# One expert step of a fused decoder trunk: transposes behind both down units, slot weights in the activations, a scatter of split values

## The chip, the cores and the metric

The kernel runs on one core of a Trainium2 chip. TensorE (PE in the profile, PEld for its weight loads) multiplies, VectorE (DVE) and ScalarE (ACT) work element by element, GpSimd (POOL) and SyncE (SP) do small things and issue transfers. The engines run each its own list of instructions in order and wait for one another through semaphores. The metric is the device time of one execution in microseconds, the median of several runs.

## The reference, cut to what matters

A decoder trunk of two layers over 256 tokens of 1024 channels. Each layer is a token mixer and a channel mixer; the channel mixer of the second layer picks two of eight experts for each token. Only this last part is changed:

```python
def moe_swiglu(h, router_w, w_gate, w_up, w_down):
    logits = (h @ router_w).astype(jnp.float32)
    top_val, top_idx = lax.top_k(logits, TOP_K)
    probs = jax.nn.softmax(top_val, axis=-1)
    combine = jnp.sum(jax.nn.one_hot(top_idx, N_EXPERTS, dtype=jnp.float32) * probs[..., None], axis=-2)
    out = jnp.zeros_like(h)
    for e in range(N_EXPERTS):
        out = out + combine[..., e:e + 1].astype(h.dtype) * swiglu(h, w_gate[e], w_up[e], w_down[e])
    return out
```

An expert has 3584 hidden channels: gate and up are 1024 x 3584, down is 3584 x 1024, all float32.

## The kernel before, in words

All weights stream from memory in units of 1 MB (128 x 2048 float32) into six slots of `raw`. A weight is used as a sum of two fp32r values: ScalarE writes the high half (`moe_hi`, L730), VectorE the rest (`moe_lo`, L1110), and TensorE multiplies high by high, high by low and low by high. Three places hold split units in the expert stage, so the high half of unit w waits until TensorE has consumed unit w-3 (`act.wait_ge(consumed, w - SPLIT)`).

One expert is one step (`expert_step` on each engine), and it has 42 units. The hidden channels are cut into seven tiles of 512 (FT = 7). A tile has two gate units, two up units (`gate_up`, L1617, 12 matmuls of 512 columns each) and two down units (`down`, L1632, 12 matmuls too). The order is: units 0 to 3 are gate and up of tile 0; units 4 to 7 are gate and up of tile 1, units 8 and 9 down of tile 0; and so on up to units 38 and 39, down of tile 5; units 40 and 41 are down of tile 6. In the code, `tile(step, r, ...)` issues gate and up of one tile and down of the tile before it.

A step has up to 128 slots, the tokens that chose the expert. `select` (L1184) builds a 0/1 matrix `sel` of tokens by slots and a matrix `sel_w` with the router's weights in it. `gather` (L1652) multiplies the tokens by `sel` into two banks of PSUM; ScalarE (`input_high`, L812) and VectorE (`split_input`, L1256) split the result into `xe_hi` and `xe_lo`. For each tile ScalarE writes Silu of the gate (`silu_tile`, L780), VectorE multiplies it by the up result (`multiply`, L1244), TensorE transposes the product (`turn`, L1642, four transposes into bank 4), and the two engines split it again (`tile_high`, L807, `split_tile`, L1249) for the down units.

At the end of a step, TensorE transposes `sel_w` (`turn_selection`, L1660), ScalarE copies it and the result of the expert (`expert_result`, L819 and L821), and two units into the next step `scatter` (L1670) multiplies the result by the turned selection, in float32, into four banks; VectorE adds them to the output (`add_result`, L1264). In each tile, TensorE's order is

```python
down(step, k + 4, 1 - odd, 0, t - 1, first=first, rounds=rounds)
turn(step, odd, t)
down(step, k + 5, 1 - odd, 1, t - 1, rounds=rounds)
```

ScalarE's order in a tile is high halves 0 and 1 of its six units, `tile_high`, high halves 2 and 3, `silu_tile`, high halves 4 and 5. VectorE's is low halves 0 and 1, `split_tile`, low halves 2 to 5, `multiply`.

Of the kernel before, what the change touches and what calls it, by code (L numbers as in the profile page):

```python
# [29 lines left out]
P = 128  # L30
# [141 lines left out]
C_RS = A_CONST + 4 * P  # L172
C_RT = C_RS + T
C_MOD = C_RT + T
# [7 lines left out]
def program(nc, x_t, vecs, glr_w, a2, router, stream, experts, out_t):  # L182
    with ExitStack() as ctx:
# [93 lines left out]
        y_e = area(A_GATES + 4096, D)  # L277
        silu_e = [area(A_GATES + 5120 + 512 * i, 512) for i in range(2)]
        act_e = [area(A_SQ + 512 * i, 512) for i in range(2)]
        sel, sel_w, sel_t = area(A_SK, T), area(A_SK + 256, T), area(A_SK + 512, T)  # L280
# [12 lines left out]
        list_f, hits = area(A_GQ + 156, 8), area(A_GQ + 164, 8)  # L293
        router_sb = area(A_GQ + 256, KC, N_EXP)
        index = sb("index", [P, 2, 8], U32)
        xe_hi, xe_lo = split_area(0, KC * P), split_area(1024, KC * P)
        ae_hi = [split_area(4096 + 1024 * b, 512) for b in range(2)]
# [61 lines left out]
        ye_copied, scattered, moe_added = sem("expert_y_copied"), sem("scattered"), sem("moe_added")  # L359
        sel_zeroed, sel_w_ready = sem("selection_zeroed"), sem("weighted_selection_ready")  # L360

# [160 lines left out]
        def _(act):  # L522
# [259 lines left out]
            def expert_step(step, expert, first=False):  # L782
# [26 lines left out]
            def input_high(step, half):  # L809

                act.wait_ge(gathered, step * 2 + half + 1)
                act.activation(xe_hi[:, 512 * half:512 * half + 512], (bank[7], bank[4])[half][:, :],  # L812
                               ACT.Copy).then_inc(xe_hi_done, 1)
# [25 lines left out]
        def _(dve):  # L839
# [353 lines left out]
            dve.memset(sel_w, 0.0).then_inc(sel_zeroed, 1)  # L1193
# [29 lines left out]
            select(0, sel, chosen_f, sel_ready)  # L1223
            link(dve.tensor_scalar(places[:, :, 8:16], ranks, float(P), None, ALU.subtract))
# [15 lines left out]
            def multiply(step, k, odd, t, rounds=0):  # L1240
# [3 lines left out]
                dve.tensor_tensor(act_e[odd], bank[2 * odd + 1][:, :], silu_e[odd],  # L1244
                                  ALU.mult).then_inc(act_done, 1)
# [5 lines left out]
            def split_input(step, half):  # L1251

                src = (bank[7], bank[4])[half]
# [3 lines left out]
                                  ALU.subtract).then_inc(xe_split, 1)  # L1257

# [7 lines left out]
            def expert_step(step, expert, first=False):  # L1266
                for k in range(3 if first else 0, 4):
                    moe_lo(step, k)
                add_result(step)
                dve.wait_ge(sel_turned, step + 1)  # L1270
                select(column_of(step), sel_w, weights_f, sel_w_ready)
                moe_lo(step, 4)
# [6 lines left out]
                select(column_of(step + 1), sel, chosen_f, sel_ready)  # L1279
# [5 lines left out]
            def tile(step, r, rounds, t, whole):  # L1285


                if whole:
                    moe_lo(step, 4 + 6 * r, rounds)
# [11 lines left out]
            add_result(over_steps(dve, expert_step))  # L1301
# [4 lines left out]
        def _(pe):  # L1306
# [297 lines left out]
            pe.wait_ge(sel_zeroed, 1)  # L1604
# [40 lines left out]
            def gather(step, half):  # L1645
# [3 lines left out]
                for c in range(4):  # L1649
                    for t in range(2):  # L1650
                        at = D * t + P * (4 * half + c)
                        mm = pe.matmul((bank[7], bank[4])[half][:, P * c:P * c + P],  # L1652
# [4 lines left out]
            def turn_selection():  # L1657

                for t in range(2):
                    mm = pe.transpose(bank[7][:, P * t:P * t + P], sel_w[:, P * t:P * t + P], ident)  # L1660
# [12 lines left out]

            def expert_step(step, expert):
# [35 lines left out]
            pe.wait_ge(xe_split, 1)  # L1710
            turn_selection()
# [95 lines left out]
```

## Time and profile before

| | |
|---|---|
| runs | 1996.08, 1994.54, 1990.96 us; median 1994.54 |
| span of the profiled execution | 1994.1 us |
| its mean granted TensorE clock | 0.962 |
| TensorE busy | 1868.0 us, 94% |
| VectorE busy | 1549.3 us, 78% |
| ScalarE busy | 1174.3 us, 59% |
| read from memory | 522.65 MB |
| the expert stage | from about 946 us to 1974 us of the span, eight steps |

The span is the time from the first to the last instruction of one execution; no time of that execution other than its span is given, and it is 0.4 us under the median of the runs. Matmuls overlap one another, so the start of one after another tells more than their durations.

### The profile page before, as it was taken

What the parts mean: (1) busy time and instruction counts of PE and PEld (TensorE: products, weight loads), DVE (VectorE), ACT (ScalarE), POOL (GpSimd) and SP (SyncE); (2) the same over time, 40 slices, a digit from 0 to 9 for tenths busy, and PEclk for the clock granted to TensorE, in tenths of its full rate; (3) what the DMA queues carried; (4) which work ended last, traced back from release to release, by engine and by line L of the source; (5) the groups of instructions that cost most, each with busy time, mean ns of one, the idle gap of its engine ahead of it and who ended that gap; (6) DMA issues with size and microseconds to landing.
All of it is one profiled execution on the core that took longest, in us unless ns stands there. A gap on an engine that the chain in (4) does not pass through costs nothing.

```text
span 1994.1 us, 29410 instructions
## 1 busy us (share of the span) xinstructions
PE 1868.0 (94%) x10996; PEld 1648.5 (83%) x10997; DVE 1549.3 (78%) x1274; ACT 1174.3 (59%) x987; POOL 196.4 (10%) x185
## 2 busy tenths in 40 slices
PE   4979998799989899997999999999999999999997
PEld 3979998799988898996888888887888878888786
DVE  6967966877656558676888888888888888888886
ACT  3347554533334476453676766767767767676674
POOL 0461601000002705010000000000000000000000
PEclk7979999899999899997999999999999999999999
DMA  8944434588634333351798998989989889898892
GB/s 351 360 167 163 171 126 169 189 322 328 259 129 148 128 120 114 129 188 64 277 368 305 369 345 328 364 317 355 364 308 364 336 337 368 304 368 336 336 364 90
DMA packets 72380, 524.81 MB, mean 263 GB/s; under 512 B 8096, under 2 KB 8224, under 8 KB 8560
## 3 DMA queue, kind: packets, MB, share of 16 engines
q1 hardware_dynamic: 72144, 523.50, 69.6%
q8 instruction: 55, 0.90, 0.2%
q0 software_dynamic: 160, 0.23, 0.0%
q14 instruction: 21, 0.17, 0.0%
HBM read 522.65 MB, written 1.05 MB: 263 GB/s over the span
## 4 chain that ended last, share of the span: by engine, by line
PE 34%; DVE 14%; ACT 5%; issue 2%; DVEq 0%; ACTq 0%
PE bank L1617 18%; DVE w_lo L1110 11%; PE bank L1632 9%; ACT w_hi L730 4%; DVE arena L1244 2%; PE bank L1642 2%; PE bank L1652 2%; PE bank L1670 2%; PE bank L1351 1%; PE bank L1328 1%; PE bank L1587 0%; DVE arena L901 0%; DVE w_lo L851 0%; DVE arena L923 0%; DVEq L1242 0%
## 5 line engine op out<-in xcount | busy, mean ns | idle before, releaser
L1110 DVE TENSOR_TENSOR w_lo<-raw,w_hi 128x2048 fp32r<-128x2048 f32 x224 | 512.9, 2290 | 83.7 <-ACT w_hi L730 62.1
L730 ACT ACTIVATE w_hi<-raw 128x2048 fp32r<-128x2048 f32 x224 | 428.5, 1917 | 127.7 <-PE bank L1632 80.0
L1351 PE MATMUL bank<-acts,w_hi 128*128 128x256 f32 x2080 | 396.1, 292 | 19.6 <-DVE acts L914 11.8
L1351 PEld LDWEIGHTS bank<-acts,w_hi 128*128 128x128 f32 x2080 | 338.0, 200 | 24.8 <-issue 14.6
L1351 PE MATMUL bank<-acts,w_lo 128*128 128x256 f32 x1040 | 301.4, 290 | 0.0
L1617 PE MATMUL bank<-acts 128*128 128x512 f32 x1248 | 300.7, 390 | 0.0
L1617 PE MATMUL bank<-w_hi,acts 128*128 128x512 f32 x960 | 297.9, 392 | 1.3 <-DVE acts L1256 1.3
L1110 DVE TENSOR_TENSOR acts<-raw,acts 128x2048 fp32r<-128x2048 f32 x112 | 256.2, 2288 | 31.3 <-ACT acts L730 28.0
L1617 PEld LDWEIGHTS bank<-acts 128*128 128x128 f32 x1248 | 233.6, 188 | 48.3
L1632 PE MATMUL bank<-w_hi,acts 128*128 128x512 f32 x832 | 261.2, 395 | 0.0
L730 ACT ACTIVATE acts<-raw 128x2048 fp32r<-128x2048 f32 x112 | 214.8, 1918 | 68.4 <-PE bank L1617 66.8
L536 ACT ACTIVATE w_hi<-raw 128x2048 fp32r<-128x2048 f32 x82 | 156.6, 1910 | 154.1 <-PE bank L1351 116.1
L851 DVE TENSOR_TENSOR w_lo<-raw,w_hi 128x2048 fp32r<-128x2048 f32 x82 | 190.7, 2326 | 68.8 <-ACT w_hi L536 66.4
L1617 PEld LDWEIGHTS bank<-w_hi,acts 128*128 128x128 f32 x960 | 179.6, 188 | 38.3 <-issue 1.5
L1351 PEld LDWEIGHTS bank<-acts,w_lo 128*128 128x128 f32 x1040 | 207.3, 199 | 0.0
L1617 PE MATMUL bank<-w_lo,acts 128*128 128x512 f32 x480 | 186.9, 389 | 0.0
L1632 PEld LDWEIGHTS bank<-w_hi,acts 128*128 128x128 f32 x832 | 152.7, 188 | 29.8
L1632 PE MATMUL bank<-w_lo,acts 128*128 128x512 f32 x416 | 162.5, 391 | 0.0
L1351 PE MATMUL bank<-acts 128*128 128x256 f32 x816 | 106.3, 292 | 5.4 <-DVE acts L851 5.4
L1351 PEld LDWEIGHTS bank<-acts 128*128 128x128 f32 x816 | 103.7, 200 | 7.0 <-DVE acts L851 5.7
L1617 PEld LDWEIGHTS bank<-w_lo,acts 128*128 128x128 f32 x480 | 90.1, 188 | 18.9
L868 DVE SCALAR_TENSOR_TENSOR arena<-raw,arena 128x2048 f32<-128x2048 f32 x42 | 99.7, 2374 | 7.7 <-DMA raw<-in_stream 4.3
(233 smaller groups left out, 2239.8 us busy)
## 6 DMA issues: line engine op xcount, KB each, us to landing
raw<-in_experts SPq DMA_DIRECT2D x336, 1024.0 KB, 4.8
raw<-in_stream SPq DMA_DIRECT2D x161, 1024.0 KB, 5.3
arena<-in_x_t SPq DMA_DIRECT2D x1, 1024.0 KB, 9.7
out_t<-arena SPq DMA_DIRECT2D x2, 512.0 KB, 2.7
arena<-in_vecs SPq DMA_DIRECT2D x1, 228.0 KB, 2.6
arena<-in_glr_w POOLq DMA_DIRECT2D x2, 64.0 KB, 4.0
arena<-in_a POOLq DMA_DIRECT2D x2, 32.0 KB, 4.0
arena<-in_router POOLq DMA_DIRECT2D x1, 32.0 KB, 2.0
```

The source lines that it names most:

```text
L536: act.activation(w_hi[SLOT[u]], raw[:, slot, :], ACT.Copy).then_inc(hi_written, 1)
L730: act.activation(w_hi[s], raw[:, slot, :], ACT.Copy).then_inc(hi_written, 1)
L851: dve.tensor_tensor(w_lo[SLOT[u]], raw[:, POS[u] % RAW, :], f32(w_hi[SLOT[u]]), ALU.subtract).then_inc(lo_written, 1)
L868: ins = dve.scalar_tensor_tensor(acc, w, cond[:, k:k + 1], acc, ALU.mult, ALU.add)
L1110: dve.tensor_tensor(w_lo[s], raw[:, slot, :], f32(w_hi[s]), ALU.subtract).then_inc(lo_written, 1)
L1244: dve.tensor_tensor(act_e[odd], bank[2 * odd + 1][:, :], silu_e[odd], ALU.mult).then_inc(act_done, 1)
L1351: mm = pe.matmul(out[:, c, :], w[:, 256 * k + P * c:256 * k + P * c + P], (hi if high else lo)[:, k, :], start=(k == 0 and n == 0 and c == 0),
L1617: mm = pe.matmul(bank[b][:, :], (xe_hi if high else xe_lo)[:, c:c + P], w[:, 512 * kk:512 * kk + 512], start=(half == 0 and kk == 0 and n ...
L1632: mm = pe.matmul(bank[5 + d][:, :], (ae_hi if high else ae_lo)[odd][:, c:c + P], w[:, 1024 * f + 512 * d:1024 * f + 512 * d + 512], start= ...
L1642: mm = pe.transpose(bank[4][:, P * c:P * c + P], act_e[odd][:, P * c:P * c + P], ident)
L1652: mm = pe.matmul((bank[7], bank[4])[half][:, P * c:P * c + P], h_tok[:, at:at + P], sel[:, P * t:P * t + P], start=(t == 0), stop=(t == 1))
L1670: mm = pe.matmul(SCATTER[p][:, T * c:T * c + T], y_e[:, d:d + P], sel_t, start=True, stop=True)
```

## The change

It has four parts, all in the expert stage.

1. `turn` of a tile stands behind both down units. The first tile of a step, whose transposes stood alone ahead of unit 4, has them behind units 4 and 5. ScalarE's `tile_high` and VectorE's `split_tile` move from behind the second unit of a tile to behind the third. VectorE makes the low half of unit 5 ahead of the first `multiply`.
2. The weights of the router are multiplied into the activations. The turned `sel_w` goes into bank 5; ScalarE makes a 0/1 matrix `sel_t` of it with Sign, VectorE sums it over the tokens into `slot_w`, one weight for each slot, and `multiply` multiplies by that too. `turn_selection` moves from the end of a step to behind the scatter of the next. `select` of the weights moves to the end of a step, next to that of `sel`.
3. The scatter works on fp32r: ScalarE writes the high half of the result, VectorE the rest (`split_result`, new), and two matmuls per 128 channels take the place of one in float32.
4. The second half of the gather goes into bank 2 and no longer waits for the last tile's split. Some small areas of memory move.

```diff
             def expert_result(step):
-                act.wait_ge(sel_turned, step + 1)
-                act.activation(sel_t, bank[7][:, 0:T], ACT.Copy).then_inc(ye_copied, 1)
+                act.wait_ge(consumed, step * EU + N_W)
                 for half in range(2):
-                    act.activation(y_e[:, 512 * half:512 * half + 512], bank[5 + half][:, :],
+                    act.activation(ye_hi[:, 512 * half:512 * half + 512], bank[5 + half][:, :],
                                    ACT.Copy).then_inc(ye_copied, 1)
...
                 silu_tile(step, 1, 0)
+                act.wait_ge(sel_turned, step + 1)
+                act.activation(sel_t[:, :], bank[5][:, 0:T], ACT.Sign).then_inc(sel_signed, 1)
                 with act.Fori(0, (FT - 1) // 2) as q:
                     for r in range(2):
                         for j in range(4):
                             moe_hi(step, 4 + 6 * r + j, q * 2)
-                            if j == 1:
+                            if j == 2:
                                 tile_high(step, r, q * 2 + r)
...
-                dve.tensor_tensor(act_e[odd], bank[2 * odd + 1][:, :], silu_e[odd],
-                                  ALU.mult).then_inc(act_done, 1)
+                dve.scalar_tensor_tensor(act_e[odd], bank[2 * odd + 1][:, :], slot_w, silu_e[odd],
+                                         ALU.mult, ALU.mult).then_inc(act_done, 1)
...
+            def split_result(step):
+                for half in range(2):
+                    c = 512 * half
+                    dve.wait_ge(ye_copied, step * 2 + half + 1)
+                    dve.tensor_tensor(ye_lo[:, c:c + 512], bank[5 + half][:, :], f32(ye_hi[:, c:c + 512]),
+                                      ALU.subtract).then_inc(ye_split, 1)
...
             def expert_step(step, expert, first=False):
-                for k in range(3 if first else 0, 4):
+                for k in range(4):
+                    if k == 2:
+                        split_result(step)
+                    if not (first and k < 3):
+                        moe_lo(step, k)
+                add_result(step)
+                dve.wait_ge(sel_signed, step + 1)
+                dve.reduce_sum(slot_w, bank[5][:, 0:T], mybir.AxisListType.X).then_inc(slot_w_ready, 1)
+                for k in (4, 5):
                     moe_lo(step, k)
-                add_result(step)
-                dve.wait_ge(sel_turned, step + 1)
-                select(column_of(step), sel_w, weights_f, sel_w_ready)
-                moe_lo(step, 4)
+                dve.wait_ge(slot_w_ready, step + 1)
                 multiply(step, 3, 0, 0)
...
-                select(column_of(step + 1), sel, chosen_f, sel_ready)
+                column = column_of(step + 1)
+                select(column, sel, chosen_f, sel_ready)
+                select(column, sel_w, weights_f, sel_w_ready)
                 split_tile(step, 0, FT - 1)
...
-                for j in range(1, 6):
+                for j in range(0 if whole else 2, 6):
                     moe_lo(step, 4 + 6 * r + j, rounds)
-                    if j == 1:
+                    if j == 2:
                         split_tile(step, r, t - 1)
...
             def scatter(step):
-                pe.wait_ge(ye_copied, step * 3 + 3)
+                pe.wait_ge(ye_split, step * 2 + 2)
...
-                        mm = pe.matmul(SCATTER[p][:, T * c:T * c + T], y_e[:, d:d + P], sel_t,
-                                       start=True, stop=True)
+                        to = SCATTER[p][:, T * c:T * c + T]
+                        pe.matmul(to, ye_hi[:, d:d + P], sel_t[:, :], start=True, stop=False)
+                        mm = pe.matmul(to, ye_lo[:, d:d + P], sel_t[:, :], start=False, stop=True)
...
                 scatter(step)
+                turn_selection(step)
                 for k in range(2):
                     gate_up(step, 2 + k, 1, k)
                 pe.wait_ge(moe_added, step * 4 + 4)
-                turn(step, 0, 0)
...
                 gather(step + 1, 0)
+                gather(step + 1, 1)
                 pe.wait_ge(ae_split, step * FT + FT)
-                gather(step + 1, 1)
                 for half in range(2):
                     down(step, EU - 2 + half, 0, half, FT - 1, last=True)
-                pe.wait_ge(xe_split, step * 2 + 3)
-                pe.wait_ge(sel_w_ready, step * 2 + 2)
-                turn_selection()
...
                 for j in range(2):
                     gate_up(step, k + j, 2 * odd, j, rounds)
+                if first:
+                    turn(step, 0, 0)
                 for j in range(2):
                     gate_up(step, k + 2 + j, 2 * odd + 1, j, rounds)
                 down(step, k + 4, 1 - odd, 0, t - 1, first=first, rounds=rounds)
+                down(step, k + 5, 1 - odd, 1, t - 1, rounds=rounds)
                 turn(step, odd, t)
-                down(step, k + 5, 1 - odd, 1, t - 1, rounds=rounds)
```

## Rows read from the trace of the kernel before

**Rows 1.** The page: span, and TensorE's busy time, share and instructions.

```profile
span 1994.1 us, 29410 instructions
...
PE 1868.0 (94%) x10996; PEld 1648.5 (83%) x10997; DVE 1549.3 (78%) x1274; ACT 1174.3 (59%) x987; POOL 196.4 (10%) x185
```

**Rows 2.** Waits, 950 to 1985: who waited for whom, us, times, longest.

```profile
PE bank L1642 <- DVE arena L1244: 16.1, 54, 0.9
```

**Rows 3.** Timeline of TensorE, a scatter and a tile: start us, us, instructions [idle before].

```profile
1208.26 3.61 PE L1670 MATMUL bank<-arena 128*128 128x256 f32 x16
1211.53 0.81 PE L1617 MATMUL bank<-w_hi,acts 128*128 128x512 f32 x2
...
1218.19 0.66 PE L1642 MATMUL bank<-arena 128*128 128x128 f32 x4 [0.86 <-DVE arena L1244]
...
1267.05 0.66 PE L1642 MATMUL bank<-arena 128*128 128x128 f32 x4 [0.23 <-DVE arena L1244]
...
1270.32 2.88 PE L1617 MATMUL bank<-acts 128*128 128x512 f32 x12
...
1281.20 0.61 PE L1632 MATMUL bank<-w_hi,acts 128*128 128x512 f32 x2
...
1284.30 0.66 PE L1642 MATMUL bank<-arena 128*128 128x128 f32 x4 [0.22 <-DVE arena L1244]
```

**Rows 4.** Timeline of TensorE, from the last transposes of a step to the next scatter.

```profile
1318.76 0.66 PE L1642 MATMUL bank<-arena 128*128 128x128 f32 x4 [0.23 <-DVE arena L1244]
1322.02 3.73 PE L1652 MATMUL bank<-arena 128*128 128x128 f32 x32
1325.51 2.98 PE L1632 MATMUL bank<-acts 128*128 128x512 f32 x12
1331.05 0.38 PE L1660 MATMUL bank<-arena 128*128 128x128 f32 x2
...
1336.74 3.61 PE L1670 MATMUL bank<-arena 128*128 128x256 f32 x16
```

**Rows 5.** Timeline of ScalarE: a high half in a tile, then around the step's end.

```profile
1281.39 1.92 ACT L730 ACTIVATE acts<-raw 128x2048 fp32r<-128x2048 f32 x1 [0.80 <-PE bank L1617]
...
1319.95 1.91 ACT L730 ACTIVATE acts<-raw 128x2048 fp32r<-128x2048 f32 x1
1321.76 1.89 ACT L730 ACTIVATE w_hi<-raw 128x2048 fp32r<-128x2048 f32 x1
...
1331.75 1.08 ACT L821 ACTIVATE arena<-bank 128x512 f32<-128x512 f32 x2
```

**Rows 6.** Timeline of VectorE around the same end of a step.

```profile
1321.89 2.29 DVE L1110 TENSOR_TENSOR acts<-raw,acts 128x2048 fp32r<-128x2048 f32 x1 [1.11 <-ACT acts L730]
...
1327.75 0.69 DVE L1256 TENSOR_TENSOR acts<-bank,acts 128x512 fp32r<-128x512 f32 x1 [0.23 <-DVE w_lo L1110]
1328.36 2.29 DVE L1110 TENSOR_TENSOR w_lo<-raw,w_hi 128x2048 fp32r<-128x2048 f32 x1
...
1339.70 2.48 DVE L1264 TENSOR_TENSOR arena<-arena,bank 128x512 f32<-128x512 f32 x4 [0.23 <-PE bank L1670]
```

**Rows 7.** Timeline of TensorE in the dense layer: fp32r matmuls of 256 columns.

```profile
644.10 0.40 PE L1351 MATMUL bank<-acts,w_hi 128*128 128x256 f32 x2
644.34 0.28 PE L1351 MATMUL bank<-acts,w_lo 128*128 128x256 f32 x1
```

**Rows 8.** A group of VectorE's by line, and the stage's table load.

```profile
L973 DVE SCALAR_TENSOR_TENSOR arena<-bank,arena 128x384 f32<-128x384 f32 x16 | 8.9, 558 | 74.0 <-ACT arena L622 74.0
...
951.21 1.28 ACT L780 ACT_TABLE_LOAD   x1
```

**Rows 9.** Two idle stretches of TensorE, and one window with its granted clock.

```profile
325.77 0.47 PE L1351 MATMUL bank<-acts,w_hi 128*128 128x256 f32 x2 [2.51 <-DVE acts L1099]
...
880.17 0.47 PE L1351 MATMUL bank<-acts,w_hi 128*128 128x256 f32 x2 [2.61 <-DVE acts L1099]
...
881.10:884.50 3.40, 3.40 (x19) 3.40 (x18) 3.22 (x6) 2.05 (x3) 0.00 (x0) 0.50 0.68 282
```

More of the change, by code:

```diff
@@ L171 @@
 C_ID, C_ONES, C_LNEG, C_NEG = (A_CONST + P * i for i in range(4))
-C_RS = A_CONST + 4 * P
+C_RS = A_ST + 1536
 C_RT = C_RS + T
-C_MOD = C_RT + T
+C_MOD = A_CONST + 4 * P
 C_VEC = C_MOD + DEPTH * 80
@@ L276, in program @@
         moe_y = area(A_GATES + 2048, KC * T)
-        y_e = area(A_GATES + 4096, D)
         silu_e = [area(A_GATES + 5120 + 512 * i, 512) for i in range(2)]
         act_e = [area(A_SQ + 512 * i, 512) for i in range(2)]
-        sel, sel_w, sel_t = area(A_SK, T), area(A_SK + 256, T), area(A_SK + 512, T)
+        sel, sel_w = area(A_SK, T), area(A_SK + 256, T)
         iota, tril = area(A_SK + 768, P), area(A_SK + 896, P)
@@ L293, in program @@
         list_f, hits = area(A_GQ + 156, 8), area(A_GQ + 164, 8)
+        slot_w = area(A_GQ + 180, 1)
         router_sb = area(A_GQ + 256, KC, N_EXP)
@@ L296, in program @@
         xe_hi, xe_lo = split_area(0, KC * P), split_area(1024, KC * P)
+        ye_hi, ye_lo = split_area(2048, D), split_area(3072, D)
+        sel_t = sb("selection_turned", [P, T], F32R)
         ae_hi = [split_area(4096 + 1024 * b, 512) for b in range(2)]
@@ L359, in program @@
         ye_copied, scattered, moe_added = sem("expert_y_copied"), sem("scattered"), sem("moe_added")
+        ye_split, sel_signed = sem("expert_y_split"), sem("selection_signed")
         sel_zeroed, sel_w_ready = sem("selection_zeroed"), sem("weighted_selection_ready")
+        slot_w_ready = sem("slot_weights_ready")
         block = ctx.enter_context(nc.Block())
@@ L811, in input_high @@
                 act.wait_ge(gathered, step * 2 + half + 1)
-                act.activation(xe_hi[:, 512 * half:512 * half + 512], (bank[7], bank[4])[half][:, :],
+                act.activation(xe_hi[:, 512 * half:512 * half + 512], (bank[7], bank[2])[half][:, :],
                                ACT.Copy).then_inc(xe_hi_done, 1)
             def expert_result(step):
-                act.wait_ge(sel_turned, step + 1)
-                act.activation(sel_t, bank[7][:, 0:T], ACT.Copy).then_inc(ye_copied, 1)
+                act.wait_ge(consumed, step * EU + N_W)
                 for half in range(2):
-                    act.activation(y_e[:, 512 * half:512 * half + 512], bank[5 + half][:, :],
+                    act.activation(ye_hi[:, 512 * half:512 * half + 512], bank[5 + half][:, :],
                                    ACT.Copy).then_inc(ye_copied, 1)
@@ L1192, in _ @@
             link(dve.memset(moe_y, 0.0))
-            dve.memset(sel_w, 0.0).then_inc(sel_zeroed, 1)
+            dve.memset(f32(sel_t[:, :]), 0.0).then_inc(sel_zeroed, 1)
             dve.wait_ge(moe_consts, 3)
@@ L1223, in _ @@
             select(0, sel, chosen_f, sel_ready)
+            select(0, sel_w, weights_f, sel_w_ready)
             link(dve.tensor_scalar(places[:, :, 8:16], ranks, float(P), None, ALU.subtract))
@@ L1251, in split_input @@
             def split_input(step, half):
-                src = (bank[7], bank[4])[half]
+                src = (bank[7], bank[2])[half]
                 c = 512 * half
@@ L1285, in tile @@
             def tile(step, r, rounds, t, whole):
-                if whole:
-                    moe_lo(step, 4 + 6 * r, rounds)
-                for j in range(1, 6):
+                for j in range(0 if whole else 2, 6):
                     moe_lo(step, 4 + 6 * r + j, rounds)
-                    if j == 1:
+                    if j == 2:
                         split_tile(step, r, t - 1)
@@ L1300, in _ @@
                 expert_step(g, g)
-            add_result(over_steps(dve, expert_step))
+            n_steps = over_steps(dve, expert_step)
+            split_result(n_steps)
+            add_result(n_steps)
             norm_out(area(A_GATES + 2048, KC, T), 1, P_F, 2 * DEPTH)
@@ L1651, in gather @@
                         at = D * t + P * (4 * half + c)
-                        mm = pe.matmul((bank[7], bank[4])[half][:, P * c:P * c + P],
+                        mm = pe.matmul((bank[7], bank[2])[half][:, P * c:P * c + P],
                                        h_tok[:, at:at + P], sel[:, P * t:P * t + P],
@@ L1655, in gather, with turn_selection @@
                 mm.then_inc(gathered, 1)
-            def turn_selection():
+            def turn_selection(step):
+                pe.wait_ge(sel_w_ready, step * 2 + 2)
                 for t in range(2):
-                    mm = pe.transpose(bank[7][:, P * t:P * t + P], sel_w[:, P * t:P * t + P], ident)
+                    mm = pe.transpose(bank[5][:, P * t:P * t + P], sel_w[:, P * t:P * t + P], ident)
                 mm.then_inc(sel_turned, 1)
             def scatter(step):
-                pe.wait_ge(ye_copied, step * 3 + 3)
+                pe.wait_ge(ye_split, step * 2 + 2)
                 pe.wait_ge(xe_split, step * 2 + 2)
```

4 lines of the change are left out of this document (1 added, 3 removed).

## The prediction

> **What bounds the kernel now.** I read the page first: TensorE is busy for 94% of the 1994.1 us span [rows 1]. An average over all stages doesn't say what a change in the last stage is worth, so the timeline of one expert step comes next. From one scatter to the next (1208.26 to 1336.74) is 128.48 us [rows 3, 4]. Four units take 10.88 us (1270.32 to 1281.20), 2.72 each [rows 3]; 42 of them are 114.2 us, 89% of the step. So TensorE sets the pace, and the rest of the step is transposes, gather and scatter, and waits. The table of waits names one wait of TensorE in this stage: the transposes of a tile wait for `multiply` (L1244), 54 times [rows 2]. In a tile it costs this much: transposes to transposes 17.25 us (1267.05 to 1284.30), less 0.41 for the transposes, 0.13 for restarting after them and 16.32 for six units, is 0.39 [rows 3]; the first two tiles lose less, so I take 2.2 for six tiles. The first transposes wait longer: two units and the wait take 6.66 us (1211.53 to 1218.19), less 5.44 and 0.20 for the restart, 1.02 [rows 3].
>
> The reader should see a second thing, which decides here. Each unit's weights are split by ScalarE (high half) and then by VectorE (low half), in strict order, two units ahead at most: `moe_hi` of unit w waits until TensorE has consumed unit w-3. A unit consumed lets the high half start 0.20 us later (1281.39, where the next unit's matmuls start at 1281.20) [rows 3, 5]; 1.92 high, 2.29 low and 0.17 of handing over make 4.58, and TensorE needs 5.44 for the two units between. The slack is 0.86 us, before anything else is put in these queues.
>
> **What the change takes away.** (a) Transposes after both down units: `multiply` gets 2.72 us more (5.44 at the first tile, whose transposes move behind two units), so the 1.02 and the 2.2 go. VectorE's work per tile then has to fit in 16.86 us: six low halves and two short operations, 15.1, with gaps of about 1.2 (some 0.2 after each low half [rows 6]), 16.35. It fits with 0.5 to spare. (b) Scatter: 3.27 us (1208.26 to 1211.53) [rows 3]. The new one is 16 fp32r matmuls of 256 columns. Such matmuls start 0.12 us apart (644.10 to 644.34 for two) [rows 7]: 1.92, a gain of 1.35 with 0.05 of restart. The six gains sum to 4.6 us per step. (c) The turned selection is only moved: two transposes, then as now a restart.
>
> **What it adds, position by position.** Zero is the start of the last tile's transposes, now 1318.76. In these queues the row after the transposes is fixed: high half of unit 40, behind `tile_high`, from +1.19 to +3.10, of unit 41 from +3.00 [rows 4, 5]. Low half of 40: +3.13 to +5.42 [rows 6]. Before, the transposes had the second down unit behind them, so unit 40 began at +6.75 (1325.51) [rows 4] and waited for nothing. After, only the gather (3.49, 1322.02 to 1325.51) stands there: TensorE is free at 0.41 + 3.49 = 3.90, and unit 40 can begin at 5.42 + 0.14 = 5.56. New wait: 1.66. The second selection (0.60 on VectorE) falls before zero, where VectorE now has 2.4 us; it costs nothing.
>
> Then VectorE has no gap for 26 us. By [rows 6], a low half is followed after 0.22, a short operation on PSUM by the next at -0.08: split of input half 0 to 6.33, low 41 to 8.54, input half 1 to 9.46, low 0 to 11.67, low 1 to 14.18. Unit 41 waits 0.30 for its low half (8.68 against 8.38) and ends at 11.40; unit 0 begins at 11.67 + 0.14 = 11.81, a wait of 0.41. ScalarE's copies of the result follow at 11.60 and end at 12.68 (two in 1.08 [rows 5]); the two new `split_result` operations, 0.69 each like those of the input [rows 6], run 14.38 to 15.68, before the scatter is due at 17.25. Low 2 to 17.89, low 3 to 20.40, four additions 20.63 to 23.11 (2.48 [rows 6]). The new `reduce_sum` over 256 columns of PSUM has no row; 512 columns take 0.69, so it is between 0 and 0.69, and I take 0.42. Low 4: 23.37 to 25.66. TensorE's side: units 0 and 1 to 17.25, scatter to 19.17, selection and restart to 19.44, units 2 and 3 to 24.88. Unit 4 begins at 25.81: a wait of 0.93. Sign itself (ScalarE, some 0.4) waits for the turned selection till about 19.6 and delays the high half of 4 to 21.8, which VectorE's 23.37 hides.
>
> The dearest comes at unit 7. `tile_high` stands in ScalarE's queue ahead of the high half of unit 7, and now waits for transposes which stand behind units 4 and 5 (25.81 to 31.25). So from the transposes' start: +1.19 high half of 7, +3.13 low half, as above [rows 5, 6], ready at 31.25 + 5.56 = 36.81. TensorE has only the transposes, a restart and unit 6 to do, till 34.51. New wait: 2.30. In the other tiles the transposes end before the tile's first unit starts, so `tile_high` is past long before the high half of its fourth unit may start, and nothing is late.
>
> Sum per step: 1.66 + 0.30 + 0.41 + 0.93 + 2.30 = 5.6 added, 4.6 taken. By positions: unit 7 at 36.81, three units to 44.97, five tiles of 16.86: the next zero at 129.27, against 128.50 now. Seven such periods: +5.5. Step 0 has no waits at units 40 and 41 of a step before it, and its first three low halves are ready; with unit 4 unhindered it comes out at +0.2. The tail: the exposed scatter is 1.35 shorter, and begins some 0.3 later, since the second split ends 2.1 after unit 41 where the copies now end at 1.78 (1332.83 against 1331.05) [rows 4, 5]: -0.9 with what follows. Total +4.7, so the span is 1998.8; the median of the runs is 0.4 above the profiled span, so **1999.2 us**, 0.24% slower. `scalar_tensor_tensor` in `multiply`: a row of one over 384 columns of PSUM takes 0.56 [rows 8], so 512 should take 0.69 to 0.8; the 0.5 of spare time per tile hides it. Moved areas and the initial second selection (0.6, beside ScalarE's copy) cost nothing; if uncovered, 0.6 once.
>
> **Rivals.** I call within 0.3% (6 us) no change; the three runs spread by 0.26%.
> *VectorE's chain is shorter than I sum (the other side).* Place: from low 40 to low 4, 22.5 us of operations and gaps, mostly queued back to back. If it were 1.2 us shorter, the waits at 41, 0 and 4 would go; the two others hang only on rows 5 and stay. Then unit 7 begins at 35.2, the period is 127.7, the time 1988. It decides from 0.8 us per step below 128.5. For it: the gaps are from one border. Against: most durations repeat to 0.01. Chance 0.12.
> *The clock falls.* Row by row: an idle stretch of 2.51 us (ending 325.77) was followed by no fall, one of 2.61 (ending 880.17) by 3.4 us at a granted clock of 0.50, that is 1.2 of 2.4 GHz [rows 9]. The wait at unit 7 shows 2.15 us idle, or 2.3 from the last start, with transposes next to it. Each fall costs half of 3.4, 1.7 us; in three steps 5, in all eight 14: 2004 to 2013. The Trainium skill (TensorE: Matmul & The Clock Gate, HAM oscillation) speaks against this change: a loop whose every round waits can re-throttle each round. The trace has that stretch at 0.50, but no fall in this stage. Chance 0.18.
> *Sign needs another table.* One load (1.28 us, 951.21) serves the whole stage now [rows 8]. Two loads per step: that at Sign is hidden, that at the next Silu comes behind the late high half of 7 and puts off units 8 and 9 by about 0.9: 7 us, 2006. Chance 0.04. The skill (ScalarE: Activation LUTs, Table sets) holds that cheap functions are filler in every set, without naming Sign in that list; if so nothing is loaded.
> *VectorE becomes the bound of a tile,* if the new multiply takes over 1.2 us. Each 0.1 beyond is 5 us: 2004 at 1.3. Chance 0.03.
> *The gain stands whole,* waits hidden: 4.6 x 8 less, 1957. It needs ScalarE to pass a waiting operation, which no row shows. Chance 0.03.
>
> **How the numbers follow.** My case has 0.60: 1999, its own range 1994 to 2004 (the reduction between 0 and 0.69 gives -3 to +2, the gaps 0.2 per step either way). Two thirds of it lie within 0.3%, one third is slower. Clock: nearly all slower. Table and multiply: slower. Shorter chain: half and half. The whole gain: faster. Faster 0.10, same 0.48, slower 0.42. The range for 8 in 10 reaches to the shorter chain and into the clock case: 1988 to 2008.
>
> **What would show it.** Period of the scatters 129.3 in place of 128.5. Transposes with no wait; five new waits of the TensorE for the low half (L1110's counterpart): some 2.3 at unit 7, 1.7 at 40, 0.9 at 4, 0.4 at 0, 0.3 at 41. ScalarE idle before the first `tile_high`. Scatter of 1.9. I am wrong if unit 7 starts with no wait, if VectorE shows gaps between low 40 and low 4, if a load stands before Sign, or if the clock row is below 1.00.

## The result, and the profile after

| | before | after |
|---|---|---|
| median of four runs | 1994.0 us (1990.96 to 1996.08) | 2002.18 us (2001.46 to 2003.86) |
| span of the profiled execution | 1994.1 us | 1999.7 us |
| scatter to scatter, one step | 128.5 us | 128.9 us, or 130.5 us with a fall of the clock |

The ratio of the times is 1.0042, with a 95% interval of 1.0028 to 1.0056: slower, by 8 us. The forecast was 1999.2 us. Up to 0.3% the prediction called it no change, and held that for a little likelier (0.48) than slower (0.42); 0.42% is beyond it, so the second came.

On the page of the kernel after, TensorE is busy for 8.5 us less than in [rows 1], although the span is 5.6 us longer: less work and more waiting.

```profile
span 1999.7 us, 29409 instructions
...
PE 1859.5 (93%) x10994; PEld 1645.9 (82%) x10995; DVE 1567.4 (78%) x1302; ACT 1172.1 (59%) x986; POOL 196.2 (10%) x185
```

The table of TensorE's waits from 950 to 1990 shows where. The line of [rows 2], 54 waits for `multiply`, is gone. In its place stand 15 waits of gate and up units (L1637) and 8 of down units (L1652), all for the low half of a weight (L1115); the third line is the wait ahead of the last scatter.

```profile
PE bank L1637 <- DVE acts L1115: 21.0, 15, 2.1
PE bank L1652 <- DVE acts L1115: 9.9, 8, 1.2
PE bank L1692 <- DVE acts L1270: 2.0, 1, 2.0
```

The timeline of TensorE answers to [rows 4], from the last transposes of a step (1319.51, the zero of the prediction) through units 40 and 41, the scatter, and on to the turn of the first tile and unit 7. In brackets is the idle time ahead of an instruction; a wait told from starts is longer than that by 0.14 to 0.25 us (unit 7: 2.23 against 2.07).

```profile
1319.51 0.60 PE L1662 MATMUL bank<-arena 128*128 128x128 f32 x4
1319.94 3.74 PE L1672 MATMUL bank<-arena 128*128 128x128 f32 x32
1324.92 3.01 PE L1652 MATMUL bank<-acts 128*128 128x512 f32 x12 [1.24 <-DVE acts L1115]
1328.04 0.73 PE L1652 MATMUL bank<-w_hi,acts 128*128 128x512 f32 x2
...
1331.14 0.73 PE L1637 MATMUL bank<-w_hi,acts 128*128 128x512 f32 x2
...
1336.72 0.28 PE L1692 MATMUL bank<-selection_turned,acts 128*128 128x256 f32 x1
...
1338.62 0.38 PE L1681 MATMUL bank<-arena 128*128 128x128 f32 x2
...
1345.13 3.02 PE L1637 MATMUL bank<-acts 128*128 128x512 f32 x12 [0.65 <-DVE acts L1115]
...
1350.72 0.60 PE L1662 MATMUL bank<-arena 128*128 128x128 f32 x4
...
1356.13 2.47 PE L1637 MATMUL bank<-acts 128*128 128x512 f32 x6 [2.07 <-DVE acts L1115]
```

All of it lands within 0.2 us of where the prediction put it, each position counted from 1319.51; only the next zero comes 0.4 earlier:

| starts at | unit 40 | 41 | 0 | scatter | unit 4 | turn | unit 7 | next zero |
|---|---|---|---|---|---|---|---|---|
| predicted | 5.56 | 8.68 | 11.81 | 17.25 | 25.81 | 31.25 | 36.81 | 129.27 |
| measured | 5.41 | 8.53 | 11.63 | 17.21 | 25.62 | 31.21 | 36.62 | 128.9 without a fall |

The scatter takes 1.90 us (1336.72 to 1338.62) against the 3.27 of [rows 3]. VectorE's timeline answers to [rows 6]. From the low half of unit 40 (1322.57) on it works through without a pause but for the 0.23 of handing over: the sum over the tokens takes 0.42, and `multiply` with its extra factor 0.75.

```profile
1317.53 1.12 DVE L1189 TENSOR_SCALAR arena<-arena 128x128 f32<-128x128 f32 x4 [0.35 <-issue]
1322.57 2.29 DVE L1115 TENSOR_TENSOR acts<-raw,acts 128x2048 fp32r<-128x2048 f32 x1 [1.11 <-ACT acts L734]
...
1340.06 2.48 DVE L1278 TENSOR_TENSOR arena<-arena,bank 128x512 f32<-128x512 f32 x4 [0.23 <-DVE w_lo L1115]
1342.46 0.42 DVE L1288 TENSOR_REDUCE arena<-bank 128x1 f32<-128x256 f32 x1
1342.80 2.28 DVE L1115 TENSOR_TENSOR acts<-raw,acts 128x2048 fp32r<-128x2048 f32 x1
...
1347.91 0.75 DVE L1250 SCALAR_TENSOR_TENSOR arena<-bank,arena 128x512 f32<-128x512 f32 x1 [0.32 <-DVE w_lo L1115]
...
1353.79 2.29 DVE L1115 TENSOR_TENSOR acts<-raw,acts 128x2048 fp32r<-128x2048 f32 x1 [1.11 <-ACT acts L734]
```

ScalarE's timeline answers to [rows 5] and holds the cause of the two dear waits. Before `tile_high` (L813) it stands idle for 6.68 and 4.91 us, though the weights behind it could have been converted in that time. The high half that TensorE needs next (L734) follows only then: of unit 40 at 1320.64, of unit 7 at 1351.85. Sign takes 0.39 us, and no table load stands before it.

```profile
1320.14 0.60 ACT L813 ACTIVATE acts<-bank 128x512 fp32r<-128x512 f32 x1 [6.68 <-PE bank L1662]
1320.64 1.90 ACT L734 ACTIVATE acts<-raw 128x2048 fp32r<-128x2048 f32 x1
...
1339.04 0.39 ACT L794 ACTIVATE selection_turned<-bank 128x256 fp32r<-128x256 f32 x1 [1.52 <-PE bank L1681]
...
1351.35 0.60 ACT L813 ACTIVATE acts<-bank 128x512 fp32r<-128x512 f32 x1 [4.91 <-PE bank L1662]
1351.85 1.91 ACT L734 ACTIVATE acts<-raw 128x2048 fp32r<-128x2048 f32 x1
```

What the likeliest case did not have is in the windows (us, busy time of PE, PEld, DVE, ACT and POOL with instructions, granted clock of TensorE, share of the DMA engines, GB/s). The first four are whole steps, from scatter to scatter; they alternate, 130.5 and 128.9, and the long ones have a clock of 0.99. The fifth shows why: for 3.40 us, from 0.6 us behind the start of unit 7 on, the granted clock is 0.50, which is 1.2 of 2.4 GHz. The sixth is the same place one step before, at 1.00.

```profile
1077.33:1207.85 130.52, 126.40 (x584) 103.94 (x583) 111.79 (x70) 89.37 (x61) 0.00 (x0) 0.99 0.89 338
1207.85:1336.72 128.87, 124.76 (x584) 102.79 (x582) 111.55 (x70) 89.35 (x61) 0.00 (x0) 1.00 0.89 342
1336.72:1467.20 130.48, 126.33 (x584) 103.93 (x582) 111.79 (x70) 89.35 (x61) 0.00 (x0) 0.99 0.87 337
1467.20:1596.13 128.93, 124.82 (x583) 102.79 (x582) 111.55 (x70) 89.36 (x61) 0.00 (x0) 1.00 0.89 342
...
1356.70:1360.10 3.40, 3.40 (x9) 2.64 (x8) 3.18 (x2) 1.13 (x1) 0.00 (x0) 0.50 0.77 275
...
1227.20:1230.60 3.40, 3.35 (x15) 2.78 (x16) 2.95 (x2) 2.06 (x2) 0.00 (x0) 1.00 0.66 183
```

There are four such falls, at 1097.3, 1356.7, 1616.1 and 1875.5, in every second of the eight steps. One costs 130.5 - 128.9 = 1.6 us.

The account of the profiled execution: from unit 0 of step 0 to the last scatter it takes 1038.5 us where it took 1029.4, which is 9.1 more. Four falls make 6.4 of it, seven periods of +0.41 make 2.9, and the first step is 0.2 shorter. Behind the last scatter it is 1.3 shorter, and the stages ahead of the experts, which the change does not touch, ended 2.2 earlier: that leaves the 5.6 between the spans. In every run with both on record a time is 1.7 to 1.9 us above its span. So the profiled execution of before took about 1995.9, above its median, and that of after 2001.46, below its own; hence 8.2 between the medians.

### The profile page after: what moved, and what is told of

The parts are those of the page before. It is cut to its first block, busy times and chain, and to the rows that moved or that the text cites. A ratio compares the mean times of both kernels' runs of the same rounds, so it can differ in the third digit from the quotient of the medians.

```text
span 1999.7 us, 29409 instructions
## 1 busy us (share of the span) xinstructions
PE 1859.5 (93%) x10994; PEld 1645.9 (82%) x10995; DVE 1567.4 (78%) x1302; ACT 1172.1 (59%) x986; POOL 196.2 (10%) x185
## 4 chain that ended last, share of the span: by engine, by line
PE 43%; DVE 9%; ACT 2%; issue 2%; DVEq 0%; ACTq 0%
PE bank L1637 26%; PE bank L1652 13%; DVE acts L1115 3%; DVE w_lo L1115 3%; ACT acts L734 2%; PE bank L1662 1%; PE bank L1372 1%; DVE arena L1278 1%; PE bank L1349 1%; PE bank L1608 0%; DVE acts L1270 0%; PE bank L1672 0%; DVE arena L906 0%; DVE w_lo L856 0%; DVE arena L928 0%
## 5 line engine op out<-in xcount | busy, mean ns | idle before, releaser
L1115 DVE TENSOR_TENSOR w_lo<-raw,w_hi 128x2048 fp32r<-128x2048 f32 x224 | 513.2, 2291 | 68.1 <-ACT w_hi L734 35.0
L734 ACT ACTIVATE w_hi<-raw 128x2048 fp32r<-128x2048 f32 x224 | 428.6, 1917 | 91.5 <-PE bank L1652 64.1
L1372 PE MATMUL bank<-acts,w_hi 128*128 128x256 f32 x2080 | 396.4, 293 | 17.7 <-DVE acts L919 11.5
L1637 PE MATMUL bank<-acts 128*128 128x512 f32 x1248 | 312.9, 400 | 21.0 <-DVE acts L1115 21.0
L1637 PE MATMUL bank<-w_hi,acts 128*128 128x512 f32 x960 | 298.2, 392 | 2.0 <-DVE acts L1262 1.5
L1637 PEld LDWEIGHTS bank<-acts 128*128 128x128 f32 x1248 | 234.7, 192 | 75.3 <-DVE acts L1115 27.4
L1115 DVE TENSOR_TENSOR acts<-raw,acts 128x2048 fp32r<-128x2048 f32 x112 | 255.9, 2285 | 25.3 <-ACT acts L734 23.5
L734 ACT ACTIVATE acts<-raw 128x2048 fp32r<-128x2048 f32 x112 | 214.8, 1917 | 80.3 <-PE bank L1637 74.3
L1652 PE MATMUL bank<-w_hi,acts 128*128 128x512 f32 x832 | 257.2, 390 | 0.7
L1637 PEld LDWEIGHTS bank<-w_hi,acts 128*128 128x128 f32 x960 | 178.4, 188 | 41.1 <-DVE w_lo L1115 3.5
L1637 PE MATMUL bank<-w_lo,acts 128*128 128x512 f32 x480 | 187.0, 390 | 0.0
L1652 PEld LDWEIGHTS bank<-w_hi,acts 128*128 128x128 f32 x832 | 155.5, 188 | 36.2 <-DVE w_lo L1115 4.0
L1652 PE MATMUL bank<-w_lo,acts 128*128 128x512 f32 x416 | 162.0, 390 | 0.0
L1637 PEld LDWEIGHTS bank<-w_lo,acts 128*128 128x128 f32 x480 | 90.1, 188 | 19.2
```

Source lines behind the costliest of these rows:

```text
L734: act.activation(w_hi[s], raw[:, slot, :], ACT.Copy).then_inc(hi_written, 1)
L1115: dve.tensor_tensor(w_lo[s], raw[:, slot, :], f32(w_hi[s]), ALU.subtract).then_inc(lo_written, 1)
L1372: mm = pe.matmul(out[:, c, :], w[:, 256 * k + P * c:256 * k + P * c + P], (hi if high else lo)[:, k, :], start=(k == 0 and n == 0 and c == 0),
L1637: mm = pe.matmul(bank[b][:, :], (xe_hi if high else xe_lo)[:, c:c + P], w[:, 512 * kk:512 * kk + 512], start=(half == 0 and kk == 0 and n ...
L1652: mm = pe.matmul(bank[5 + d][:, :], (ae_hi if high else ae_lo)[odd][:, c:c + P], w[:, 1024 * f + 512 * d:1024 * f + 512 * d + 512], start= ...
```

## The experiments

Two theories were to be told apart. *The queue*: the conversion of units 40 and 7 stands behind `tile_high` and `split_tile`, which now wait for later transposes; all else the change does is small or a gain. *Rivals*: the new work on VectorE (sum, low halves of the result) sets the pace, or the clock's falls, and not the waits themselves, are the loss. The kernels are the one after with the edits shown, unless another is named.

**Unit 7 first.** In the first tile, ScalarE converts unit 7 ahead of `tile_high` and VectorE ahead of `split_tile`. (`high_tile(r, q, j)` is the body of ScalarE's loop over a tile, with `tile_high` behind its high half j.)

```diff
+                high_tile(0, 0, 3)
+                high_tile(1, 0, 2)
+                with act.Fori(1, (FT - 1) // 2) as q:
+                    for r in range(2):
+                        high_tile(r, q, 2)
...
-                    if j == 2:
+                    if j == (2 if whole else 3):
                         split_tile(step, r, t - 1)
```

> Changed kernel, with one order altered in the first tile of a step: ScalarE writes the high half of unit 7 ahead of the first tile_high, and VectorE its low half ahead of the first split_tile. Queue theory (the loss comes from halves that wait behind the moved transposes): the wait of 2.2 us before unit 7 goes, nothing takes its place, period of a step 126.9 us without any fall of the clock, time about 1979. Clock theory (the waits are covered by what the change takes away, and only the four falls of the clock cost): the falls go, 6 us less, about 1996. Chain theory (VectorE's added operations are the bound): the wait reappears before units 8 to 10, about 1996 to 2000.

Measured: 1977.81 us, ratio to the kernel before 0.9927 [0.9910, 0.9944]. In its timeline unit 7 (1215.92) follows unit 6 with no wait; the one at unit 4 is as it was.

```profile
1207.12 3.06 PE L1642 MATMUL bank<-acts 128*128 128x512 f32 x12 [0.60 <-DVE acts L1120]
...
1212.73 0.60 PE L1667 MATMUL bank<-arena 128*128 128x128 f32 x4
...
1215.92 2.88 PE L1642 MATMUL bank<-acts 128*128 128x512 f32 x12
```

In its table of waits, those for low halves are one fewer per step:

```profile
PE bank L1657 <- DVE acts L1120: 9.9, 8, 1.2
PE bank L1642 <- DVE acts L1120: 4.4, 7, 0.6
```

The whole periods, from the scatter of the second step on, lie between 126.6 and 126.8; a step with a fall would stand out by 1.6, and none does. They are 2.2 less than 128.9, which is the whole wait of 2.23 from starts. Eight times 2.23 and the four falls, 6.4, are 24.2; the medians differ by 24.4. The kernel before was measured anew with each round of runs (1994.0 with the kernel after, 1993.1 with this one); by the distance from it the difference is 23.5. The wait at unit 7 comes from the order in the queue, and with it the falls went from the steps. One fall is left outside them, at the last scatter (1955.52).

**Unit 40 first.** The same at the step's end.

```diff
-                tile_high(step, 0, FT - 1)
-                for half in range(2):
-                    moe_hi(step, EU - 2 + half)
+                moe_hi(step, EU - 2)
+                tile_high(step, 0, FT - 1)
+                moe_hi(step, EU - 1)
...
-                split_tile(step, 0, FT - 1)
-                for half in range(2):
-                    moe_lo(step, EU - 2 + half)
-                    split_input(step + 1, half)
+                moe_lo(step, EU - 2)
+                split_tile(step, 0, FT - 1)
+                moe_lo(step, EU - 1)
+                for half in range(2):
+                    split_input(step + 1, half)
```

> Changed kernel, with one order altered at the end of a step: ScalarE writes the high half of unit 40 ahead of the last tile_high, VectorE its low half ahead of the last split_tile, and both splits of the input follow unit 41. Queue theory: the waits before units 40, 41 and 0 (1.3, 0.3 and 0.2 us) go, the one before unit 4 stays near 1, the one before unit 7 stays at 2.2, and with it some falls of the clock; period 126.6, with a fall 128.2; time about 1984. Chain theory: VectorE has the same work, so the waits gather before unit 4 and the time stays near 2000.

Measured: 1976.90 us, ratio 0.9917 [0.9897, 0.9937]; period 126.37. The waits at units 40, 41 and 0 (1.5, 0.26 and 0.23) are gone, which is 2.0; what is left of the 2.5 is the restart behind each of them and a slightly shorter way to unit 4. The waits at units 4 and 7 stand as before: 15, at most 2.1 us. The line of its table of waits:

```profile
PE bank L1638 <- DVE acts L1115: 19.5, 15, 2.1
```

Yet no step has a fall of the clock, which had been expected to stay in some: all whole periods are 126.33 to 126.37. So an idle time of 2.07 us at unit 7 does not bring a fall by itself.

**Both first.** Both edits together.

> Both alterations of order together in the changed kernel. Queue theory: period 124.4, one wait of about 1 us before unit 4 is left, clock row at 1.00, time about 1960. Clock theory: about 1996. Chain theory: VectorE's work of a step (about 120 us with its gaps) is no bound, so at most the waits before units 4 to 10 grow; above 1975 would speak for it.

Measured: 1958.51 us, ratio 0.9829 [0.9810, 0.9848]; period 124.15. By the distance from the kernel before in its own round, the two edits save 23.5 and 24.4 us of the kernel after alone and 42.8 together. The 5.1 between the sum and the pair are the four falls, 6.4, which each of them alone already removes, less the one fall, some 1.2, that all three have at the last scatter and the kernel after has not. One wait per step is left, at unit 4; its line in the table of waits:

```profile
PE bank L1643 <- DVE acts L1120: 3.1, 7, 0.6
```

and its place in the timeline:

```profile
1327.53 3.03 PE L1643 MATMUL bank<-acts 128*128 128x512 f32 x12 [0.43 <-DVE acts L1120]
```

**A filler at unit 7.** Five matmuls of no use, of data that are there, fill TensorE's wait between units 6 and 7; the orders stay.

```diff
-                for j in range(2):
-                    gate_up(step, k + 2 + j, 2 * odd + 1, j, rounds)
+                gate_up(step, k + 2, 2 * odd + 1, 0, rounds)
+                if first:
+                    for _ in range(5):
+                        pe.matmul(bank[7][:, 0:T], ident, sel[:, :], start=True, stop=True)
+                gate_up(step, k + 3, 2 * odd + 1, 1, rounds)
```

> Changed kernel with five float32 matmuls of 256 columns (about 2.0 us) into an unused bank between units 6 and 7 of each step, where TensorE waits 2.2 us anyway; nothing reads them. If the clock falls because TensorE idles there, no fall is left in the expert stage and every period is 128.9: 6 us less than the changed kernel, about 1996. If the falls come from something else in the step, they stay, and the time stays at 2002. If waits and not falls make the loss, the time is above that of before by 1 to 3 us all the same.

Measured: 1996.05 us, ratio 1.0012 [1.0000, 1.0024]; whole periods of 128.85 to 128.94, which is the shorter of the two periods after, so no step has a fall. Unit 7 starts 5.41 behind the transposes (1349.87 to 1355.28), as it did after (1350.72 to 1356.13): the fillers (L1726) cost nothing.

```profile
1344.29 3.01 PE L1637 MATMUL bank<-acts 128*128 128x512 f32 x12 [0.60 <-DVE acts L1115]
...
1349.87 0.60 PE L1662 MATMUL bank<-arena 128*128 128x128 f32 x4
...
1353.06 2.32 PE L1726 MATMUL bank<-arena 128*128 128x256 f32 x10
1355.28 3.02 PE L1637 MATMUL bank<-acts 128*128 128x512 f32 x12
```

All 11 of its executions, 1990.72 to 1998.36, are below the lowest of the kernel after, 2001.46. This gives the price of the falls, about 6 us of the 8.2; without them the change is worth +0.12%, with an interval from 0 to 0.24%. That the filling took the falls away, and not a change in when the stretch comes, is likely but not shown: "unit 40 first" has the same stretch unfilled eight times and no fall either.

**Transposes alone.** The kernel before with part 1 of the change only.

```diff
                 down(step, k + 4, 1 - odd, 0, t - 1, first=first, rounds=rounds)
-                turn(step, odd, t)
                 down(step, k + 5, 1 - odd, 1, t - 1, rounds=rounds)
+                turn(step, odd, t)
...
-                            if j == 1:
+                            if j == 2:
                                 tile_high(step, r, q * 2 + r)
```

> Kernel before with only part 1 of the change: transposes behind both down units, of the first tile behind units 4 and 5, with the orders of ScalarE and VectorE that belong to it. Scatter in float32, the router's weights in the selection, gather as before. Queue theory: the seven waits of the transposes go (3.2 us), waits come before units 40, 41 and 0 (2.0) and 7 (2.3), none before unit 4 since VectorE lacks the new operations and the scatter is long; period about 129.1 without a fall, and some falls of the clock after the wait at unit 7: 1998 to 2004. Rival (the moved transposes are the gain, the split scatter and the slot weights the loss): 1970 to 1975.

Measured: 2003.38 us, ratio 1.0044 [1.0029, 1.0059]; period 129.25, with a fall in two of the eight steps (one period of 130.8, and the last step). Both dear waits are there in its table of waits, none at unit 4:

```profile
PE bank L1616 <- DVE acts L1110: 16.6, 8, 2.1
PE bank L1631 <- DVE acts L1110: 9.9, 8, 1.2
```

In its timeline, the wait at unit 7:

```profile
1229.96 2.34 PE L1616 MATMUL bank<-acts 128*128 128x512 f32 x9 [2.07 <-DVE acts L1110]
```

**Scatter and weights alone.** The kernel after with the transposes in their old places.

> Changed kernel with the transposes where they were before (between the down units, of the first tile ahead of unit 4), and the orders of ScalarE and VectorE that belong to that. Queue theory: the scatter's 1.35 us less are mostly eaten by VectorE's two splits and the sum, since the first transposes wait 1.9 instead of 1.0; period about 128.0, no fall of the clock, the tail 1 us shorter: 1988 to 1991. Rival (this part is the loss): above 2000.

Measured: 1988.32 us, ratio 0.9972 [0.9962, 0.9982]; period 127.95, no fall. Parts 2 to 4 are a gain of 0.55 per step where the scatter alone is 1.37 shorter. Half of it comes back at the first transposes of a step, which now wait 1.54 where they waited 0.86 [rows 3]; its timeline there:

```profile
1213.60 0.65 PE L1661 MATMUL bank<-arena 128*128 128x128 f32 x4 [1.54 <-DVE arena L1250]
```

**The orders without parts 2 and 3.** The kernel before with part 1 and both altered orders, so with the old scatter and weights.

> Kernel before with part 1 of the change and the two altered orders (high half of unit 7 ahead of the first tile_high, of unit 40 ahead of the last), but float32 scatter and weighted selection as before. Queue theory: no wait before units 40, 0, 4 and 7 is left; period about 124.7, against 124.2 with the split scatter and slot weights, whose gain is largely lost in the wait before unit 4; time about 1963. Rival (slot weights and split scatter give their 1.35 us per step when nothing is late): 11 us above the version with both, 1970.

Measured: 1966.47 us, ratio 0.9866 [0.9846, 0.9886]; period 124.95, and TensorE waits for VectorE nowhere in the steps. That is about midway between what the two theories gave. With parts 2 to 4 it is 1958.5 (both first): against the kernel before of each round (1994.5 and 1993.1) they are worth 6.6 us, 0.8 in each whole period and the rest in the first and last step, although they bring the wait at unit 4 with them.

**The additions spread.** Both first, and an attempt at that last wait: only one of the four additions stands ahead of the low half of unit 4, the other three and the sum behind it. TensorE waits for the first addition ahead of unit 4 and for all four ahead of the transposes.

```diff
-                add_result(step)
-                dve.wait_ge(sel_signed, step + 1)
-                dve.reduce_sum(slot_w, bank[5][:, 0:T], mybir.AxisListType.X).then_inc(slot_w_ready, 1)
-                for k in (4, 5):
-                    moe_lo(step, k)
+                add_result(step, (0,))
+                moe_lo(step, 4)
+                add_result(step, (1, 2, 3))
+                dve.wait_ge(sel_signed, step + 1)
+                dve.reduce_sum(slot_w, bank[5][:, 0:T], mybir.AxisListType.X).then_inc(slot_w_ready, 1)
+                moe_lo(step, 5)
```

> Changed kernel with both altered orders, and the additions of the scatter spread: the first before the low half of unit 4, the others behind it, TensorE waiting for the first before unit 4 and for all before the transposes. The wait before unit 4 (0.7) goes. If VectorE is the bound from unit 41 to unit 6, the wait reappears before units 5 or 6 and the time stays within 3 us of the version with both orders (1958); if not, 6 us less, 1952.

Measured: 1964.36 us, ratio 0.9853 [0.9836, 0.9870]; period 124.80. By the distance from the kernel before in its own round that is 4.4 us worse than both first, and outside what was expected either way. The wait did not go, it moved from unit 4 to unit 5 and grew, from 0.43 to 1.04 us idle. In its table of waits:

```profile
PE bank L1644 <- DVE w_lo L1120: 8.2, 8, 1.0
```

and in its timeline:

```profile
1210.31 0.74 PE L1644 MATMUL bank<-w_hi,acts 128*128 128x512 f32 x2 [1.04 <-DVE w_lo L1120]
```

VectorE's timeline shows what came in:

```profile
1328.13 2.29 DVE L1120 TENSOR_TENSOR acts<-raw,acts 128x2048 fp32r<-128x2048 f32 x1 [0.71 <-ACT acts L734]
```

VectorE now comes to the low half of unit 4 so early that its high half is not there: ScalarE writes that from 1326.19 on, behind Sign (1325.91), which itself waits for the turned selection. In "both first" VectorE came to it behind the additions and the sum and did not wait. It loses these 0.71 us, and the low half of unit 5, behind the same work, ends 11.5 us after the start of the scatter where it ended 10.7 after it. So the order of ScalarE's queue, Sign ahead of the high half of unit 4, stands in the way; no run moves Sign.

## Why the prediction was right, and where it was off

- **The new waits.** Right in place, order and releaser: 2.23 at unit 7, 1.5 at unit 40, 0.79 at unit 4, 0.26 and 0.23 at 41 and 0, together 5.0 where 5.6 was forecast. The step "0.14 of handing over" from a low half to TensorE was too large: the low half of unit 40 ends at 1324.86 and the unit starts at 1324.92, so 0.06. It entered the waits at units 40, 41, 0, 4 and 7 alike. The cause of four of them, the place in the queue, is shown by moving the conversions alone: the two altered orders took 42.8 us off. The wait at unit 4 stays with both; it stands at the end of VectorE's unbroken run of work.
- **What it takes away.** Right: no transposes of a tile wait for `multiply` any more, and the scatter is 1.37 shorter (forecast 1.35). Waits of 5.0 and a period longer by 0.41 leave 4.6 taken away, as forecast. "Less 0.41 for the transposes" was 0.35 for the five tiles with units behind them.
- **The period.** Forecast +0.77 (129.27 against 128.50), measured +0.41 without a fall. The difference is the two terms above, 0.19 at unit 7 and 0.07 less in each of five tiles behind it, less a restart behind unit 7 that the sum had at nothing (8.30 from unit 7 to the next transposes, forecast 8.16). The prediction's other sum, 5.6 added and 4.6 taken, gives 1.0 and not 0.77; it went by the positions. Seven times 0.77 is 5.4, not 5.5; its total of 4.7 is that of 5.4.
- **The sizes that the trace did not show.** The sum over 256 columns took 0.42, as taken between 0 and 0.69; `multiply` 0.75, between 0.69 and 0.8. Nothing in a tile waited for the latter.
- **The tail.** Forecast -0.9, measured -1.3 behind the last scatter.
- **The clock.** Here the likeliest case failed. It forecast no fall and reached its 1999 with too large a period; without falls the change measures 1996.05 (the filler, with 1993.1 for the kernel before in its round). The rival "the clock falls" named the place, the wait at unit 7, and the price, 1.7 us against 1.6 measured. It came true in four steps of eight, between its bounds of three and all, but on the smaller period, so that it ended at 2002 and not from 2004 on. The step at fault is the reading of [rows 9]: one stretch of 2.51 us without a fall was taken to speak against falls at 2.15. That same stretch, in code that no kernel here changes, was followed by a fall in the trace of the kernel after (the rows stand below). The Trainium skill (TensorE: Matmul & The Clock Gate, HAM oscillation) has it that a loop which waits in every round can re-throttle in every round, and shows it on a kernel whose waits are some 3 to 5 us; here waits of 2.07 us were followed by a fall every second time.
- **The rivals that fell.** No table load stands before Sign. VectorE's chain from the low half of 40 to that of 4 is not 1.2 shorter: unit 4 begins 0.19 before its forecast place. A tile is not bound by `multiply`. The gain does not stand whole in this change; with both orders altered, the kernel is 34.6 us faster than before, where 37 were named.

That the forecast of 1999.2 lies 3 us from the median is in part luck: the periods were forecast 0.36 too long, seven times, the first step and the tail 0.4 too long each, and 6.4 us of falls were left out.

What stays open is why the clock falls in some steps and not in others. In the steps, falls came in the two kernels that wait both at unit 40 and at unit 7 (four of eight steps after, two of eight with the transposes alone), and in none of the steps of "unit 40 first", with the same 2.07 us at unit 7, nor of "unit 7 first", with the wait at unit 40. That looks like a joint effect of the two waits, but two other places speak against it. One is the stretch of 2.51 us of [rows 9], in unchanged code: no fall near it before and with the transposes alone, a fall in the other eight traces (within 0.6 us of its end in six of them, 1.4 to 1.6 us behind it in two). The other is the wait of 2.01 us ahead of the last scatter: a fall in "both first", which has neither the wait at unit 40 nor that at unit 7, and none in "the additions spread", which ends its last step in the same order, nor in the kernel after, which has both waits.

```profile
326.24 0.77 PE L1372 MATMUL bank<-acts,w_hi 128*128 128x256 f32 x2 [2.51 <-DVE acts L1104]
325.90:329.30 3.40, 3.06 (x14) 3.09 (x15) 3.31 (x7) 0.77 (x2) 0.00 (x0) 0.50 0.81 275
...
1936.90 0.38 PE L1698 MATMUL bank<-selection_turned,acts 128*128 128x256 f32 x1 [2.01 <-DVE acts L1275]
1938.45:1941.85 3.40, 3.40 (x13) 2.86 (x12) 1.70 (x3) 3.38 (x5) 0.00 (x0) 0.50 0.00 0
...
1944.32 0.38 PE L1699 MATMUL bank<-selection_turned,acts 128*128 128x256 f32 x1 [2.01 <-DVE acts L1275]
1945.80:1949.20 3.40, 3.36 (x19) 2.85 (x18) 1.77 (x3) 3.37 (x5) 0.00 (x0) 1.00 0.00 0
```

(The first two are of the kernel after, the next two of "both first", the last two of "the additions spread"; in each pair the instruction with its idle time, then a window with its granted clock.) So the same instructions with the same idle time are followed by a fall or by none. A matter of when in some cycle of the chip's the stretch falls fits all of this; no run moves a stretch in time and leaves the rest, so it is not shown.

## What to carry to other kernels

A producer moved behind more work drags along everything that stands behind its consumer in an in-order queue: for each operation that now waits longer, look at the next one in its queue, and put it ahead if its own input is already there. Here the move alone costs 0.4%, and the same move with two conversions put ahead of the waiting operation gains 1.3%. The same question goes to the operation that is moved ahead: a low half put ahead of three additions found its own high half not yet written, and the wait of TensorE moved by one unit and grew from 0.43 to 1.04 us.

## What the runs showed of the hardware

- Idle stretches of TensorE of 2.07 us, 31 us after one of 1.24, were followed by 3.4 us at half the clock in four steps of eight, and in the other four by nothing. One of 2.51 us in unchanged code was so in eight traces of ten, one of 2.01 us ahead of the last scatter in two of five. Neither the length of the stretch nor the order of the instructions decides here.
- With such a stretch filled by five float32 matmuls of 256 columns, unit 7 began no later and none of the eight steps had a fall: about 6 us back for no useful work.
- Two fp32r matmuls of 256 columns in place of one in float32 took 1.90 us for 16 where 3.27 went for 8.
